# Sampling y from the old SSD state with one hand-over a chunk, and keeping the decay matrices in their PSUM banks

## What is computed

```
# prompt, chunks of 128 tokens, for head j of group g
decay[t, s] = exp(cum[t] - cum[s])  for s <= t
y_intra[t]  = sum_s (C[t] . B[s]) decay[t, s] dt[s] x[s]
# samples, one token: h0 is the state that comes in
h_new[p, n] = h0[p, n] * exp(dt A) + dt x[p] * B[n]
y[p]        = sum_n h_new[p, n] * C[n]
```

```
y[p] = exp(dt A) * sum_n h0[p, n] C[n]  +  dt x[p] * sum_n B[n] C[n]
```

## Time and profile before

| | us |
|---|---|
| median of 3 runs | 1820.42 |
| fastest, slowest of them | 1817.92, 2899.74 |
| the profiled execution | 1819.49 |
| its span, first to last instruction | 1817.8 |
| PE busy in the span | 1734.5 (95%) |
| DVE busy | 1371.3 (75%) |
| ACT busy | 1052.1 (58%) |
| POOL busy | 139.5 (8%) |

### The profile page before, as it was taken

How to read it: one execution, slowest core, us unless ns; L and a number is a source line. 1 busy time by engine, 2 the same in 40 slices (tenths; PEclk the granted TensorE clock), 3 DMA queues, 4 the chain that set the end, 5 groups by cost and what they waited for, 6 DMA issues and landing times.

```text
span 1817.8 us, 24173 instructions
## 1 busy us (share of the span) xinstructions
PE 1734.5 (95%) x9024; PEld 1453.0 (80%) x9024; DVE 1371.3 (75%) x1379; ACT 1052.1 (58%) x1006; POOL 139.5 (8%) x135
## 2 busy tenths in 40 slices
PE   7999899999998989799999999999999999999995
PEld 5867799999786779678788788788788787887884
DVE  3668766664356875588888888888888888888885
ACT  2535444443243543377776777766776767776763
POOL 2055100000105510000000000000000000000000
PEclk9999899999999999799999999999999999999998
DMA  8455255646545525289899899899899998998990
GB/s 249 136 182 174 78 186 162 185 137 183 161 138 181 174 82 182 81 314 367 312 364 356 315 357 352 322 360 348 325 354 333 346 354 316 359 357 311 362 357 33
DMA packets 257027, 465.45 MB, mean 256 GB/s; under 512 B 8492, under 2 KB 108196, under 8 KB 256928
## 3 DMA queue, kind: packets, MB, share of 16 engines
q1 hardware_dynamic: 250288, 442.20, 70.3%
q0 software_dynamic: 6384, 21.28, 3.4%
q10 hardware_dynamic: 288, 1.08, 0.2%
HBM read 453.70 MB, written 11.15 MB: 256 GB/s over the span
## 4 chain that ended last, share of the span: by engine, by line
PE 83%; DVE 10%; ACT 2%; issue 2%; POOL 2%; DMA 1%; DVEq 0%; ACTq 0%; POOLq 0%
PE bank L853 81%; PE bank L857 2%; DVE arena L1642 2%; DVE arena L1645 2%; DVE w_lo L1645 1%; DVE moe_arena L1642 1%; DVE fw_lo L1645 1%; DVE cs_t L1645 1%; DMA arena<-in_state_ssd 1%; ACT fw_hi L1316 1%; ACT arena L1316 1%; POOL sam_tmp L742 1%; DVE arena L1847 0%; POOL sam_tmp L733 0%; DVE arena L1872 0%
## 5 line engine op out<-in xcount | busy, mean ns | idle before, releaser
L1645 DVE TENSOR_TENSOR w_lo<-wring,w_hi 128x2048 fp32r<-128x2048 f32 x336 | 768.2, 2290 | 118.2 <-ACT w_hi L1316 117.2
L1316 ACT ACTIVATE w_hi<-wring 128x2048 fp32r<-128x2048 f32 x336 | 643.4, 1918 | 254.7 <-PE bank L853 254.6
L853 PE MATMUL bank<-w_hi,xg_hi 128*128 128x512 f32 x896 | 359.6, 401 | 10.6 <-DVE w_lo L1645 9.0
L853 PE MATMUL bank<-w_lo,xg_hi 128*128 128x512 f32 x896 | 355.2, 396 | 0.0
L853 PE MATMUL bank<-w_hi,xg_lo 128*128 128x512 f32 x896 | 352.7, 394 | 0.0
L853 PE MATMUL bank<-hn,wring 128*128 128x264 f32 x1152 | 271.9, 394 | 6.6 <-DVE hn L1642 6.5
L853 PEld LDWEIGHTS bank<-hn,wring 128*128 128x128 f32 x1152 | 221.0, 194 | 50.9 <-issue 12.5
L853 PEld LDWEIGHTS bank<-w_hi,xg_hi 128*128 128x128 f32 x896 | 168.3, 188 | 51.2 <-DVE w_lo L1645 12.6
L853 PEld LDWEIGHTS bank<-w_lo,xg_hi 128*128 128x128 f32 x896 | 168.2, 188 | 40.9
L853 PEld LDWEIGHTS bank<-w_hi,xg_lo 128*128 128x128 f32 x896 | 168.4, 188 | 38.7
L1645 DVE TENSOR_TENSOR fw_lo<-wring,fw_hi 128x2048 fp32r<-128x2048 f32 (+1 forms) x54 | 113.1, 2095 | 87.6 <-ACT fw_hi L1316 87.6
(11 more groups left out here) (241 smaller groups left out, 2116.1 us busy)
## 6 DMA issues: line engine op xcount, KB each, us to landing
wring<-in_moe_w_gate SPq DMA_DIRECT2D x112, 1024.0 KB, 5.2
wring<-in_moe_w_up SPq DMA_DIRECT2D x112, 1024.0 KB, 5.2
wring<-in_moe_w_down SPq DMA_DIRECT2D x112, 1024.0 KB, 5.0
wring<-in_w_in SPq DMA_DIRECT2D x36, 1024.0 KB, 5.3
wring<-in_w_out SPq DMA_DIRECT2D x16, 1024.0 KB, 5.3
wring<-in_ffn_w_gate SPq DMA_DIRECT2D x11, 1024.0 KB, 5.5
wring<-in_ffn_w_up SPq DMA_DIRECT2D x11, 1024.0 KB, 5.3
wring<-in_ffn_w_down SPq DMA_DIRECT2D x16, 704.0 KB, 4.7
```

The source lines that it names most:

```text
L853: return nc.tensor.matmul(out, lhsT, rhs, start=start, stop=stop)
L1316: return nc.scalar.activation(out, in_, fn, **kw)
L1645: return V.tensor_tensor(out, in0, in1, op)
```

## The change

Two edits and what they need.

1. Each chunk is handed over once. POOL's `chunk(l, q)` computes the term and, from the state before its update, the product with C, into a tile of its own (`term` in `sam_tmp`, `prod_early` inside `seg` for chunks 0 to 2, `prod_late` for the others). DVE updates the state and then sums 128 columns a row, in one place of a step (`CHUNK_AT`). POOL stores chunk q - 1 at the start of `chunk(l, q)`. The halving add goes. With chunk 0 DVE computes B C once (`sam_cb`), with chunk 7 it scales the sums and adds the second part.
2. `cum` stays in its bank: DVE subtracts in place, ACT takes Exp in place, DVE's multiply reads the bank, writes `seg`, and only then frees the bank, one step later than before. PE waits for that evacuation in place of `seg_done`.
3. Banks are dealt anew for xtok, sin, btok, cb, state, rows, yT and ysam, and rows 1 is flipped behind xl tile 7 with rows 2 to 4.

```diff
-ADVANCE_AT = {("xl", 3): 0, ("xl", 5): 1, ("xl", 7): 2, ("gate", 1): 3, ("gate", 2): 4, ("gate", 3): 5, ("gate", 5): 6,
-              ("gate", 6): 7}
-SUM_AT = {("xl", 4): 0, ("xl", 6): 1, ("gate", 0): 2, ("gate", 2): 3, ("gate", 4): 4, ("gate", 5): 5, ("gate", 7): 6,
-          ("gate", 8): 7}
+CHUNK_AT = {("xl", 4): 0, ("xl", 6): 1, ("gate", 0): 2, ("gate", 1): 3, ("gate", 2): 4, ("gate", 3): 5, ("gate", 4): 6,
+            ("gate", 6): 7}
+EARLY_CHUNKS = 3
+XTOK_BANKS = (Q1, Q2, Q3, Q0)
...
-                        pl.add(Q1 + 2 * c + h, "xtok", l, c, h)
+                        pl.add(XTOK_BANKS[2 * c + h], "xtok", l, c, h)
...
-                pl.add(Q0, ("sin", "btok", "cb")[m - 2], l)
+                pl.add((Q4, Q1, Q2)[m - 2], ("sin", "btok", "cb")[m - 2], l)
...
-                        pl.add(Q1 + 2 * c + g, "state", l, c, g)
+                        pl.add(XTOK_BANKS[2 * c + g], "state", l, c, g)
...
-                    pl.add(Q1 + i, "yT", l, i)
+                    pl.add(XTOK_BANKS[i], "yT", l, i)
...
+            def chunk(l, q):
+                n = STATE_CHUNKS * l + q
...
+                st = states[q % STATE_BUFS]
+                if q == EARLY_CHUNKS - 1:
+                    b, k = fill("state", l, NC - 1, GROUPS - 1)
+                    pool.wait_ge(full[b], k + 1)
+                    load_states(l, q)
+                if n:
+                    pool.wait_ge(st_new, n)
+                if q:
+                    pool.dma_start(st_view(ssd_s, l, q - 1), states[(q - 1) % STATE_BUFS]
+                                   ).then_inc(st_stored[(q - 1) % STATE_BUFS], 16)
                 pool.wait_ge(st_landed[q % STATE_BUFS], 16 * chunk_count(l, q))
                 dx = sam_in[:, ROWS_P * q:ROWS_P * q + ROWS_P].unsqueeze(2).broadcast_to([P, ROWS_P, NS])
+                nc.gpsimd.tensor_tensor(term, dx, sam_b, ALU.mult).then_inc(tmp_ready, 1)
+                if n:
+                    pool.wait_ge(sum_ready, n)
+                nc.gpsimd.tensor_tensor(prod_of(q), st, sam_c, ALU.mult).then_inc(prod_ready, 1)
+                if q and q - 1 + STATE_BUFS < STATE_CHUNKS:
+                    pool.wait_ge(st_stored[(q - 1) % STATE_BUFS], 16 * chunk_count(l, q - 1))
+                    load_states(l, q - 1 + STATE_BUFS)
...
-                    pe.wait_ge(seg_done, 8 * l + 2 * i + 2)
+                    evacuated("cum", l, 2 * i)
+                    evacuated("cum", l, 2 * i + 1)
...
-                        evacuated("cum", l, m - 1)
-                        f(seg[:, 2 * m - 2:2 * m], seg[:, 2 * m - 2:2 * m], ACT.Exp).then_inc(segexp_ready, 1)
+                        act.wait_ge(seg_diff, 8 * l + m)
+                        diff = bank[fill("cum", l, m - 1)[0]][:, :]
+                        f(diff, diff, ACT.Exp).then_inc(segexp_ready, 1)
...
+            def sample_states(l, phase, m):
+                if (phase, m) not in CHUNK_AT:
+                    return
+                q = CHUNK_AT[phase, m]
...
+                if q == 0:
+                    evacuated("sin", l)
+                    both = cs_t.rearrange("p a m b -> p (a m b)")[:, 0:NS]
+                    link(tt(both, sam_in[:, HD:HD + NS], sam_in[:, HD + NS:HD + 2 * NS], ALU.mult))
+                    link(V.reduce_sum(sam_cb[:, :], both, AX.X))
+                dve.wait_ge(tmp_ready, n + 1)
+                dve.wait_ge(prod_ready, n + 1)
+                stt(st, st, sam_in[:, HD + 2 * NS:HD + 2 * NS + 1], term).then_inc(st_new, 1)
+                ins = V.reduce_sum(sam_y[:, ROWS_P * q:ROWS_P * q + ROWS_P], prod_of(q), AX.X)
+                if q < STATE_CHUNKS - 1:
+                    ins.then_inc(sum_ready, 1)
+                else:
+                    link(ins)
+                    link(V.tensor_scalar(sam_y[:, :], sam_y[:, :], sam_in[:, HD + 2 * NS:HD + 2 * NS + 1], None, ALU.mult))
+                    stt(sam_y[:, :], sam_in[:, 0:HD], sam_cb[:, :], sam_y[:, :]).then_inc(sum_ready, 1)
...
-                        if m == 5:
-                            dve.wait_ge(rows_out, 64 * (l + 1))
                         for i in range(2):
                             h = 2 * m + i
                             for c in range(NC):
-                                ins = V.tensor_scalar(seg[:, h, c, :], out[:, i * TP + c * Q:i * TP + (c + 1) * Q],
-                                                      tok[:, 3 * c + 1, h:h + 1], 0.0, ALU.subtract, ALU.min)
-                        evacd(ins, "cum", l, m)
+                                v = out[:, i * TP + c * Q:i * TP + (c + 1) * Q]
+                                ins = V.tensor_scalar(v, v, tok[:, 3 * c + 1, h:h + 1], 0.0, ALU.subtract, ALU.min)
+                        ins.then_inc(seg_diff, 1)
...
-                        v = seg[:, 2 * m - 2:2 * m]
-                        tt(v, v, cbm[:, :, g, :].unsqueeze(1).broadcast_to([P, 2, NC, Q]), ALU.mult
-                           ).then_inc(seg_done, 1)
+                        decay = bank[fill("cum", l, m - 1)[0]].rearrange("p (h c t) -> p h c t", h=2, c=NC)
+                        evacd(tt(seg[:, 2 * m - 2:2 * m], decay,
+                                 cbm[:, :, g, :].unsqueeze(1).broadcast_to([P, 2, NC, Q]), ALU.mult), "cum", l, m - 1)
```

More of the change, by code:

```diff
@@ L145, in plan_fills @@
                     for g in range(GROUPS):
-                        pl.add(Q1 + 2 * c + g, "state", l, c, g)
+                        pl.add(XTOK_BANKS[2 * c + g], "state", l, c, g)
             if m == 6:
[L148 to L151, removed]
+                pl.add(BN, "rows", l, 0)
+        for i in range(1, 5):
+            pl.add(XTOK_BANKS[i - 1], "rows", l, i)
         for m in range(XT):
@@ L170, in plan_fills @@
                     pl.add(Q2 + i, "hrows", l, i)
-                pl.add(Q0, "ysam", l)
+                pl.add(Q4, "ysam", l)
                 pl.add(BN, "lru_norm", l)
@@ L281, in trunk @@
         sam_y = sb("sam_y", [P, HD])
+        sam_cb = sb("sam_cb", [P, 1])
         pair_id = sb("pair_id", [P, HD])
@@ L380, in trunk, with prod_of @@
         htf = carve(HEADS * HD)
-        prods = [t.rearrange("p (r n) -> p r n", n=NS) for t in (sam_tmp[:, :], htf)]
+        term = sam_tmp.rearrange("p (r n) -> p r n", n=NS)
+        at_top = at[0]
+        at[0] = seg_at + HEADS // 4 * NC * Q
+        prod_early = carve(ROWS_P, NS)
+        at[0] = at_top
+        prod_late = htf.rearrange("p (r n) -> p r n", n=NS)
+        def prod_of(q):
+            return prod_early if q < EARLY_CHUNKS else prod_late
         assert at[0] <= 27200, at[0]
@@ L722, in load_states @@
                                ).then_inc(st_landed[q % STATE_BUFS], 16)
[L724 to L730, removed]
+            def chunk(l, q):
+                n = STATE_CHUNKS * l + q
+                sam_b, sam_c = (sam_in[:, HD + i * NS:HD + (i + 1) * NS].unsqueeze(1).broadcast_to([P, ROWS_P, NS])
+                                for i in range(2))
+                st = states[q % STATE_BUFS]
[8 more added lines that the diff above has]
+                                   ).then_inc(st_stored[(q - 1) % STATE_BUFS], 16)
@@ L779, in _ @@
                 pool.wait_ge(evac[b], n + 1)
[L780 to L787, removed]
+                for q in range(EARLY_CHUNKS):
+                    chunk(l, q)
                 for i in range(5):
@@ L799, in _ @@
                                ).then_inc(final_out, 16)
[L800 to L809, removed]
+                for q in range(EARLY_CHUNKS, STATE_CHUNKS):
+                    chunk(l, q)
+                q = STATE_CHUNKS - 1
+                pool.wait_ge(st_new, STATE_CHUNKS * (l + 1))
+                pool.dma_start(st_view(ssd_s, l, q), states[q % STATE_BUFS]).then_inc(st_stored[q % STATE_BUFS], 16)
                 for i in range(2):
@@ L1048, in _ @@
                     if m == 6:
-                        for i in range(2):
-                            conv_rows(l, i)
-                for i in range(2, 5):
+                        conv_rows(l, 0)
+                for i in range(1, 5):
                     if i == 4:
@@ L1387, in _ @@
                     if m == 7:
-                        for i in range(2):
-                            keep_rows(i)
-                for i in range(2, 5):
+                        keep_rows(0)
+                for i in range(1, 5):
                     keep_rows(i)
@@ L1442, in ssd_squares @@
                     f(xc[:, 4 * g:4 * g + 4, :], ysz[:, 4 * g:4 * g + 4, :], ACT.Square).then_inc(ysq_ready, 1)
-                act.wait_ge(seg_done, 8 * (l + 1))
+                for m in range(XT - 4, XT):
+                    evacuated("cum", l, m)
                 for m in range(XT):
```

20 lines of the change are left out of this document (4 added, 16 removed).

## The result

The changed kernel takes 1795.33 us, median of 4 runs (1790.60 to 1795.87); the kernel before takes 1819.17 beside it. One of the four runs of the kernel before took 2899.74 us and is left out of the ratio. The ratio is 0.9866, with a 95% interval from 0.9843 to 0.9889: 24 us, 1.3%, faster. Three repeats of the same program gave 1793.73, 1794.43 and 1794.42. The forecast was 1792, in a range from 1788 to 1806. The profiled execution took 1795.45 us, with a span of 1793.8 (before: 1819.5 and 1817.8).

A forecast was written before the change was run, and what follows sets the result against it. TensorE, 83% of the chain, waited for VectorE twice a layer (10.1 and 10.7 us) and ran slow afterwards. Removing this was to gain 14.2 us a layer: 1819.5 - 28.2 = 1791.3, stated as 1792, range 1788 to 1806.

The forecast's parts named there:

- The main step: Mixer of each layer: shorter POOL rounds and chunk 2's move remove TensorE's waits for VectorE; 14.2 us a layer.
- both waits: TensorE waiting for VectorE in layer 0: 3.84 us before the gate products, 6.23 us before the fourth yT; both nearly vanish.
- slow stretches: TensorE at lowered clock behind each wait in layer 0: 2.3 us lost after the first, 2.2 after the second.
- The replay of DVE's gate loop: Step-by-step timing of VectorE's gate steps 1 to 8 in layer 0; last multiply done at 176.9, fourth yT at 177.0.
- In place in PSUM: Differences and Exps writing PSUM banks: taken as no extra cost, with up to 9 us kept for the range.
- the second wait's 11.95 us: Layer 0's fourth yT was to start at 177.0 in place of 188.95.
- POOL's round behind an update: GpSimd's store issue, term and product after VectorE's state update: 0.60 + 1.89 + 2.37 and gaps, 5.0 us.
- nothing is given back: Behind z tile 3, VectorE's and ScalarE's parts move as much as TensorE, so the gain is kept whole.
- B: Rival: lock only moves from multiply to factors, wider reduction eats the add, TensorE waits as before; 1815 to 1821, chance 0.07.
- A: Rival: one of the two waits stays, through shifted POOL products or dear PSUM writes; 1796 to 1807, chance 0.30.
- C: Rival: hand-over becomes a chain, with late loads making VectorE wait five times a gate loop; 1835, chance 0.04.

The follow-up runs named there:

- The late Sqrt: Changed kernel with ScalarE's Sqrt moved from gate step 6 to step 7, behind the copy of gate tile 7 and the Exp: 1793.30 us, ratio 0.9857 to before.
- the banks alone: Kernel before with only the decay matrices kept in their PSUM banks, hand-overs and bank numbers as before: 1817.56 us, ratio 0.9988.
- at chunk 2: Changed kernel with chunk 2's hand-over back at the end of xl step 7, before the conv of the samples: 1812.06 us, ratio 0.9957 to before.
- at the halving add: Changed kernel with POOL again adding the two halves of each product and DVE summing 64 columns a row: 1807.81 us, ratio 0.9935 to before.
- the hand-over run: Changed kernel with the decay matrices back in SBUF, so only the single hand-over remains: 1797.20 us, ratio 0.9876 to before.

## Why the prediction was right

**The main step was right.** It said that both waits would go with their slow stretches, because POOL would have a shorter round a chunk and chunk 2 would leave the sample conv's way. Put on the start of the state products, the second gate round of layer 0 starts 6.0 us earlier (predicted 6.1): 133.61 - 118.50 = 15.11 before, 128.66 - 119.59 = 9.07 after. In layer 1 it is 5.9 for 6.4. The experiments bear out both causes: chunk 2 back in its old place costs 18 to 20 us, the add 13 to 14. These are prices of going back from the changed kernel and not shares of the gain; they add up to more than the whole, because chunk 2's old place beside POOL's new order gives PE a first wait of 7.83 us, twice the 3.84 of before. No run parts the product from the old state from the rest of the hand-over.

**The replay of DVE's gate loop held in its shape and ran 0.6 us fast.** It had 1.1, 2.1 and 2.1 us of standing in steps 3 to 5; the rows show 1.98, 2.96 and 3.02 against 0.70, so 1.3, 2.3 and 2.3. It had the last multiply start at 176.3 and end at 176.9; on the clock of before (less 1.09) it starts at 176.87. The reduction takes 1.21 us, 1.13 to the next start, as estimated.

**In place in PSUM costs nothing**, the value taken. Four differences take 1.13 us, as they did towards SBUF, and the Exp 0.59, against 0.62 in SBUF before:

```profile
143.57 0.62 ACT L1316 ACTIVATE arena<-arena 128x512 f32<-128x512 f32 x1
```

The Trainium skill, VectorE: DVE Perf Modes, section on the TRN2 errata, would have the multiply from a bank longer by 0.065 us, an estimate from its cycles. The multiply takes 0.68 with the bank and took 0.69 without, so the runs don't show it.

**The term that was too large** is the second wait's 11.95 us. The fourth yT starts 59.29 us after the state products, 11.2 earlier than before; the replay had it at 177.0 - 118.5 = 58.5. The size that failed is POOL's round behind an update, taken as 5.0 us. In step 3 DVE's update gives way to the next instruction here, and POOL's product for the next chunk ends at 156.63, 5.14 later:

```profile
151.49 1.21 DVE L1723 TENSOR_REDUCE sam_y<-arena 128x8 f32<-128x1024 f32 x1
```

In step 2 it is 5.15 and in step 4 5.21. (The replay's 142.0 + 5.0 = 146.9 should read 147.0; nothing hangs on it.) Three rounds in a row hold up the factors, so each hands its 0.15 to 0.2 us on, and the last multiply is 0.57 late.

A second thing was left out. The replay had DVE's last factor of step 5 at 165.4 (166.96 - 1.09 = 165.9 measured), but I didn't take it on to ScalarE's queue, where Sqrt waits for it with gate tile 7's copy behind. So PE waits 1.21 us before z tile 1 and not 0.4 at yT. The late Sqrt shows what this is worth: without it the fourth yT starts 173.99 - 114.84 = 59.15 us after the state products. Of the 0.8 us that were missed, 0.65 are DVE's and 0.14 the queue's.

Behind the fourth yT "nothing is given back" held: z tiles and yT regain 2.56 us in layer 0 for the 2.2 predicted, as z tiles 2 and 3 take 7.23 where tiles 0 and 1 took 7.53 before. So a part of what the fourth yT missed was made up here, which nothing in the prediction foresaw. In sum 13.7 for 14.2 in layer 0; layer 1 gives 13.3 for 14.0.

**What is left of the difference.** The mixers have 27.0 us against 28.2; the other 3.0 of the profiled execution lie outside them and come and go between executions of the same program.

**Rivals.** B had the lock move from the multiply to the factors, and it does, as the prediction noted; and the banks alone give only 1.6 to 3.1 us, so by that part B was right, and it was wrong in that the rest of the change gives 23. A's price was of the right kind: what brings POOL back by one add costs 13 us. C did not occur: among DVE's waits in the two mixers there is none for POOL.

**What I had too small in the experiments** were the prices of lateness: at chunk 2 and at the halving add I expected about half. At chunk 2 the missing part was the conv's standing through chunk 3's two POOL instructions. At the add it was the wait at z tile 1 (4.92 us, expected 3.5) and TensorE's slow stretch behind it.

## What to carry to other kernels

When VectorE stands for GpSimd, taking one instruction out of the way moves the standing to the next one with two SBUF inputs; what paid here was fewer GpSimd instructions and a release at a time when VectorE has only one-input or PSUM work. Replay the late engine's loop step by step with prices to the next start, and take the other engine's round from row to row, not as a sum of its instructions: 0.15 us a round, three rounds long, was most of what this replay missed. Then follow each time that moves into every queue that waits for it, here ScalarE's. Compare by the distance between two fixed rows of the trace: it repeated to 0.04 us here, where medians scattered by 1.6.

## What the runs showed of the hardware

- A DVE instruction that stands ends after POOL's by its own time alone less some 0.14 us: 0.09 us after it with 64 columns (0.23 alone; 120.09 + 5.28 = 125.37, POOL's product until 125.28), 0.55 to 0.58 with 512 or 528 (0.69 or 0.70 alone; 0.58 in the changed kernel, 0.56 in the hand-over run, where the product ended at 154.88 and the multiply at 155.44).
- Two POOL instructions whose records overlap (a term and its product) are not parted by it: the multiply of the hand-over run began while the term ran and stood through both. A gap of 0.08 us between POOL's product and add was enough for DVE to get in. POOL's add then took 1.62 us, and 1.27 where no DVE instruction got in the earlier trace rows. Why the conv step recorded at 120.09 stood for POOL's term at 121.08 stays open.
- A TensorE wait of 4.9 us before z tile 1 was followed by a tile of 6.43 us in place of 3.83 in layer 0, of 6.02 in layer 1. One of 3.04 us was followed by 5.51 in layer 0 and by the full-speed 3.83 in layer 1. One of 1.21 us was never followed by a slow tile.
- ScalarE's Exp from bank to bank takes 0.58 to 0.59 us, 0.03 less than in SBUF. The Trainium skill, ScalarE: Activation LUTs, "Step-by-step: what each stage is for", has ScalarE faster towards PSUM. The row agrees, but it reads from a bank as well, so it can't say which side the 0.03 us come from.
